# Prompt logits: the low keys of two key chunks in the two partition halves, multiplied by 64 rows each

## The chip, the cores and the metric

The kernel runs on one core of a Trainium2 chip. The metric is the device time of one execution in microseconds; runs of one kernel here lie within 3 us of each other. The engines are named as in the profile: PE (TensorE, matrix products), PEld (its weight loads), DVE (VectorE), ACT (ScalarE), POOL (GpSimd) and SP (SyncE, which here only issues transfers).

## What is computed

One inference step of a decoder layer on a prompt of 2048 tokens and on 8 sample sequences of 4 tokens. The stage that the change touches is stick-breaking attention over the prompt, 8 heads of 64:

```python
def stick_breaking(q, k, v, sb_bias, q_pos, k_pos):
    z = jnp.einsum('bqhd,bkhd->bhqk', q.astype(jnp.float32), k.astype(jnp.float32)) * (HEAD_DIM_SB ** -0.5)
    z = z + sb_bias.astype(jnp.float32)[None, :, None, None]
    mask = k_pos[None, :] < q_pos[:, None]
    log_1mb = jnp.where(mask, jax.nn.log_sigmoid(-z), 0.0)
    suffix = lax.cumsum(log_1mb, axis=3, reverse=True) - log_1mb
    a = jnp.where(mask, jnp.exp(jax.nn.log_sigmoid(z) + suffix), 0.0)
    o = jnp.einsum('bhqk,bkhd->bqhd', a, v.astype(jnp.float32))
    return o.astype(v.dtype)
```

Before it stand the projections to q, k, v and the gated MLP group; after it the output projection, the convolutional feed-forward layer and a per-layer embedding, all in float32.

## The kernel before

Matrix products whose accuracy matters are made of parts: an operand x is split into a high part, x rounded to float32r (a type of 4 bytes that PE multiplies in one pass), and a low part, x minus the high part, also float32r. Elsewhere in the kernel a product is high·high + high·low + low·high (`split_product`, lines 58 to 60).

The kernel is four functions one after the other: `project_mlp`, `project_qk`, `attend` (line 701) and `finish_tokens` (line 1326). `project_qk` writes the transposed queries and keys QT and KT to memory; `attend` writes its result MIXT, which `finish_tokens` loads first.

`attend` runs over 128 steps: 8 heads (`s // NQ`) times 16 query blocks of 128 queries (`s % NQ`, called i). Block i sees 128·(i+1) keys. Keys are taken in granules of up to 1024, which fill one of two PSUM buffers `ps_z` of two banks; blocks 0 to 7 have one granule, blocks 8 to 15 two. Within a granule, chunks of 512 keys (`BANK`) go to one bank each. A chunk narrower than 256 is widened to 256.

How the logits use the 128 rows of PE: a head has only 64 dimensions, so the keys lie twice in the partitions, rows 0 to 63 and again 64 to 127 (`k_hi`, `k_lo`, both 128 x 2048, one slot for each of two heads). `q2` holds the high part of the queries in rows 0 to 63 and the low part in rows 64 to 127. So one product of q2 with k_hi (line 966) gives both high·high and low·high, and one with k_lo (line 967) gives high·low and low·low. Where the chunk holds the diagonal block, a small bf16 product of the identity with a mask (line 970) adds -2^100 to the keys that are not seen. Each matmul has its own load of the 128 query columns as weights.

A step on the engines: PE makes the logits of block t (`logits`), then ACT two sigmoids of each granule (lines 1112 and 1114, into `beta` and `rest`), DVE a running product over the keys (line 1232) and the weights (line 1237); PE transposes the weights of block t-3 (`turn`, line 976), ACT copies them out (`take`, line 1101) and PE multiplies them by V (`weigh`, line 988). Between these, PE does the attention of the sample sequences in units spread over the steps by their estimated cost (`units_of`): transposes of pages of K (line 998), their logits in four column strips of the array (line 1008, `tile_position=(0, 32 * bi)`), and products with pages of V in four column strips (line 1041). POOL loads the pages as PE frees them.

Every engine has its order written out in the program; they meet by semaphores. On PE, `logits` waits for `b_done` (the sigmoids of two granules earlier), and for `half_ready` at blocks 0 (4 in the first head) and 8.

The operands are made for half a head (1024 tokens, number n) at a time. SP loads `k_raw` and `q_raw`, each twice, one copy in each partition half, after `half_ready` reaches n; ACT rounds the keys (`keys_high`); DVE does three parts in three successive steps, beginning with block 10 of the head before (first half) or block 4 of the same head (second half): part 0 rounds the queries (line 1206), part 1 subtracts to make the low rows (line 1209), part 2 makes the low keys (line 1214) and raises `half_ready`. The first 512 tokens of head 0 are made apart (`first_operands`, lines 1222 to 1227).

Of the kernel before, what the change touches and what calls it, by code (L numbers as in the profile page):

```python
# [6 lines left out]
F32R = mybir.dt.float32r  # L7
I32 = mybir.dt.int32
ALU = mybir.AluOpType
# [3 lines left out]
P = 128  # L13
BANK = 512
# [29 lines left out]
def f32(ap):  # L44

    return ap.bitcast(F32)
# [654 lines left out]
def attend(nc, keep, T, D):  # L701
# [10 lines left out]
    HALF, FIRST = 1024, BANK  # L712
# [6 lines left out]
    def keys_of(s):  # L719
        return P * (s % NQ + 1)  # L720
# [4 lines left out]
    def granule(s, g):  # L725
        return sum(granules[:s]) + g
# [56 lines left out]
    for t in range(STEPS + LAG + 1):  # L783
        s = t - LAG
# [6 lines left out]
    with ExitStack() as ctx:  # L791
        m = Alloc(nc, ctx, "at")
        k_raw, q_raw = m.sb("k_raw", [P, HALF]), m.sb("q_raw", [P, HALF])
        k_hi, k_lo, q2 = ([m.sb(f"{n}{s}", [P, 2048], F32R) for s in range(2)] for n in ("k_hi", "k_lo", "q2"))
        v = [m.sb(f"v{s}", [P, NQ, 64]) for s in range(2)]
        beta = [m.sb(f"beta{s}", [P, 2048]) for s in range(3)]
        rest = [m.sb(f"rest{s}", [P, 2048]) for s in range(4)]
# [4 lines left out]
        far_b, ident_b = m.sb("far_b", [P, P], BF16), m.sb("ident_b", [P, P], BF16)  # L802
# [18 lines left out]
        loaded, k_high, q_high, half_ready, z_ready, b_done, product_done, a_done = (  # L821
            m.sem(n) for n in ("loaded", "k_high", "q_high", "half_ready", "z_ready", "b_done", "product_done", "a_done"))
        o_ready, o_out, made, cast, rest_zeroed = (m.sem(n) for n in ("o_ready", "o_out", "made", "cast", "rest_zeroed"))
        first_loaded, first_k_high, first_q_high, first_ready, summed = (
            m.sem(n) for n in ("first_loaded", "first_k_high", "first_q_high", "first_ready", "summed"))
# [41 lines left out]
        with nc.Block() as block:  # L867
# [72 lines left out]
            def _(pe):  # L940
# [7 lines left out]
                def logits(s, g):  # L948
                    i, h = s % NQ, s // NQ
                    n = keys_of(s)  # L950
                    if s == 0:
                        pe.wait_ge(first_ready, 1)
                    if i == (4 if h == 0 else 0) and g == 0:
                        pe.wait_ge(half_ready, 2 * h + 1)
                    if i == 8 and g == 0:
                        pe.wait_ge(half_ready, 2 * h + 2)
                    at = granule(s, g)
                    z = ps_z[at % 2]
                    pe.wait_ge(b_done, at + 1)
                    width = min(n - 1024 * g, 1024)  # L960
                    for c in range(0, width, BANK):
                        w = max(min(BANK, width - c), 2 * P)
                        k0 = 1024 * g + c
                        diagonal = k0 <= n - P < k0 + w
                        q = q2[h % 2][:, i * P:(i + 1) * P]
                        nc.tensor.matmul(z[:, c:c + w], q, k_hi[h % 2][:, k0:k0 + w], start=True, stop=False)
                        last = nc.tensor.matmul(z[:, c:c + w], q, k_lo[h % 2][:, k0:k0 + w], start=False, stop=not diagonal)  # L967
                        if diagonal:
                            d = n - P - 1024 * g
                            last = nc.tensor.matmul(z[:, d:d + P], ident_b[:, :], far_b[:, :], start=False, stop=True)  # L970
                    last.then_inc(z_ready, 1)

                def turn(s, r):
# [103 lines left out]
                for t in range(STEPS + LAG + 1):  # L1077
                    s = t - LAG
                    for g, u in units_of[t]:
                        sample_turns(g, u)  # L1080
                    if has(s):
                        pe.wait_ge(a_done, s + 1)
                        for r in range(first_turns(t)):
                            turn(s, r)
                    if has(t):
                        for g in range(granules[t]):
                            logits(t, g)
                    if has(s):
                        for r in range(first_turns(t), groups[s]):
                            turn(s, r)  # L1090
                    if has(s - 1):
                        weigh(s - 1)
                    for g, u in units_of[t]:
                        sample_products(g, u)
# [104 lines left out]
            def _(dve):  # L1199
                def operands(n, part, first=0):  # L1200
                    slot = n // 2 % 2
                    src = slice(first, HALF)
                    cols = slice(n % 2 * HALF + first, n % 2 * HALF + HALF)
                    if part == 0:
                        dve.wait_ge(loaded, 64 * n + 64)
                        nc.vector.tensor_copy(q2[slot][:, cols], q_raw[:, src]).then_inc(q_high, 1)
                    if part == 1:
                        dve.wait_ge(q_high, n + 1)
                        nc.vector.tensor_tensor(q2[slot][64:P, cols], q_raw[64:P, src], f32(q2[slot][64:P, cols]), ALU.subtract)
                        if n % 2 == 0 and n:  # L1210
                            biases_of(n // 2)
                    if part == 2:
                        dve.wait_ge(k_high, n + 1)
                        nc.vector.tensor_tensor(k_lo[slot][:, cols], k_raw[:, src], f32(k_hi[slot][:, cols]), ALU.subtract).then_inc(half_ready, 1)

                def biases_of(h):
                    nc.vector.tensor_scalar(bias[h % 2][:, :], keep["sb_bias"][:, h:h + 1], 1.0, None, ALU.mult)
                    nc.vector.tensor_scalar(minus_bias[h % 2][:, :], keep["sb_bias"][:, h:h + 1], -1.0, None, ALU.mult)

                def first_operands():  # L1220
                    dve.wait_ge(first_loaded, 64)
                    nc.vector.tensor_copy(q2[0][:, 0:FIRST], q_raw[:, 0:FIRST]).then_inc(first_q_high, 1)
                    biases_of(0)
                    dve.wait_ge(first_q_high, 1)
                    nc.vector.tensor_tensor(q2[0][64:P, 0:FIRST], q_raw[64:P, 0:FIRST], f32(q2[0][64:P, 0:FIRST]), ALU.subtract)
                    dve.wait_ge(first_k_high, 1)
                    nc.vector.tensor_tensor(k_lo[0][:, 0:FIRST], k_raw[:, 0:FIRST], f32(k_hi[0][:, 0:FIRST]), ALU.subtract).then_inc(first_ready, 1)

                def product(s):
                    r = rest[s % 4][:, 0:keys_of(s) - 1][:, ::-1]  # L1230
# [76 lines left out]
                dve.wait_ge(made, 2)  # L1307
                nc.vector.tensor_copy(far_b[:, :], far[:, :]).then_inc(cast, 1)
                first_operands()
                for t in range(STEPS + LAG + 2):  # L1310
                    for g, u in units_of[t]:
                        sample_unit(g, u)
                    if has(t - 1):
                        product(t - 1)
                    if has(t - 2):
                        weights(t - 2)
                    for g, u in units_of[t - 1] if t else ():
                        sample_sums(g, u)
                    if t == 1:
                        for part in range(3):  # L1320
                            operands(0, part, FIRST)
                    for half in range(2):
                        part, h = t % NQ - PART_AT[half], t // NQ + 1 - half
                        if 0 <= part < 3 and h < HEADS:
                            operands(2 * h + half, part)
# [644 lines left out]
def program(nc, T):  # L1970

    D = {n: nc.dram_tensor(n, s, F32, kind="Internal").ap() for n, s in
         (("XT", (1024, 2080)), ("PT", (256, 2080)), ("MIXT", (1024, 2080)), ("QT", (512, 2048)), ("KT", (512, 2048)))}
    with ExitStack() as ctx:
        m = Alloc(nc, ctx, "keep")
        keep = {
            "ident": m.sb("ident", [P, P]), "mean1024": m.sb("mean1024", [P, P]), "mean512": m.sb("mean512", [P, P]),
            "eps": m.sb("eps", [P, 1]), "cols": m.sb("cols", [P, P]), "rs": m.sb("rs", [P, 17]),
            "page_table": m.sb("page_table", [1, P], I32), "sb_bias": m.sb("sb_bias", [P, 8]),
            "qT_s": m.sb("qT_s", [P, 4, 32]), "kT_s": m.sb("kT_s", [P, 4, 32]),  # L1980
        }
        project_mlp(nc, keep, T, D)
        project_qk(nc, keep, T, D)
        attend(nc, keep, T, D)
        finish_tokens(nc, keep, T, D)
# [27 lines left out]
```

## Time and profile before

| | |
|---|---|
| median of 3 runs | 3334.49 us (3333.34 to 3336.3) |
| the profiled execution | 3333.62 us |
| its span in the profile | 3331.6 us |
| mean granted clock of PE in it | 0.982 |
| PE busy | 3181.0 us, 95% |
| DVE busy | 2066.9 us, 62% |
| ACT busy | 1679.9 us, 50% |
| `attend` on PE | 587 to 1330 us of the span |

Times in the profile are microseconds from the start of the span. A row of the view by order of time gives the start, how long the row's instructions take together, engine, line, operation, output and inputs, the shape of the array used (rows*columns), the shape of the streamed operand and the number of instructions run together in the row. PE's matmuls are pipelined: one starts while the one before is still in its tail, so that the distance between starts says what a matmul costs, and the duration says more than that.

### The profile page before, as it was taken

The numbers are of one execution on the slowest core, as the hardware profiler recorded it, in microseconds if no ns is written. First come the engines' busy times: TensorE is split into PE (matmuls) and PEld (weight loads), VectorE is DVE, ScalarE is ACT, GpSimd is POOL, SyncE is SP. The second block draws the span as 40 slices with busy tenths as digits, with TensorE's granted clock in tenths as the row PEclk, the third lists the DMA queues.
The fourth block names the chain that finished last, engine by engine and source line by source line (L and its number), as shares of the span: only waits on it lengthen the run. The fifth ranks groups of instructions, "written<-read, shape, count | busy, mean of one in ns | idle before, by whom it ended". The sixth has DMA issues, their size and how long they took to land.

```text
span 3331.6 us, 52003 instructions
## 1 busy us (share of the span) xinstructions
PE 3181.0 (95%) x18462; PEld 2929.8 (88%) x18462; DVE 2066.9 (62%) x2823; ACT 1679.9 (50%) x2411; POOL 148.3 (4%) x277
## 2 busy tenths in 40 slices
PE   8999899898899889799999999999999999999997
PEld 6888687787678777799999999999999999999997
DVE  4222322777767777577477764777557775678745
ACT  5343211887768767454345443545445543454433
POOL 0000000210311111000000000000000000000000
PEclk9999999999999999899999999999999999999999
DMA  5322333642644333644445334543335433444341
GB/s 170 99 91 74 111 111 101 169 124 74 182 135 122 105 106 97 180 117 118 117 138 149 113 115 116 151 141 113 114 105 178 126 113 116 139 128 119 115 116 59
DMA packets 577751, 405.50 MB, mean 122 GB/s; under 512 B 38025, under 2 KB 539186, under 8 KB 577554
## 3 DMA queue, kind: packets, MB, share of 16 engines
q1 hardware_dynamic: 535172, 298.70, 31.4%
q0 software_dynamic: 20544, 67.19, 7.0%
q10 hardware_dynamic: 21872, 37.39, 3.3%
q8 instruction: 108, 1.77, 0.2%
q14 instruction: 55, 0.45, 0.0%
HBM read 358.34 MB, written 44.87 MB: 121 GB/s over the span
## 4 chain that ended last, share of the span: by engine, by line
PE 57%; ACT 1%; DVE 1%; issue 1%; DMA 0%; ACTq 0%; DVEq 0%
PE pf_acc L60 19%; PE pf_acc L58 19%; PE pf_acc L59 18%; PE pf_ps_sum L1457 0%; DMA pf_mix<-MIXT 0%; ACT pf_c L1635 0%; ACT pf_sq L1582 0%; ACTq L1640 0%; PE pf_ps_t L1494 0%; ACT pf_w_hi L1575 0%; DVE pf_h L1937 0%; DVE pf_u L1744 0%; DVE pf_h L1760 0%; DVE pf_ssum L1754 0%; PE pf_ps_t L1564 0%
## 5 line engine op out<-in xcount | busy, mean ns | idle before, releaser
L60 PE MATMUL pf_acc<-pf_x_hi,pf_w_lo 128*128 128x416 f32 x2080 | 734.2, 353 | 0.0
L1575 ACT ACTIVATE pf_w_hi<-pf_raw 128x1024 fp32r<-128x1024 f32 x440 | 464.6, 1057 | 534.1 <-PE pf_acc L60 528.4
L58 PE MATMUL pf_acc<-pf_x_hi,pf_w_hi 128*128 128x416 f32 x2080 | 732.0, 352 | 1.6 <-issue 0.9
L59 PE MATMUL pf_acc<-pf_x_lo,pf_w_hi 128*128 128x416 f32 x2080 | 725.9, 349 | 0.0
L1738 DVE TENSOR_TENSOR pf_w_lo<-pf_raw,pf_w_hi 128x1024 fp32r<-128x1024 f32 x440 | 536.9, 1221 | 266.6 <-ACT pf_w_hi L1575 266.4
L58 PE MATMUL pf_acc<-pf_f_hi,pf_w_hi 128*128 128x416 f32 x1280 | 454.8, 355 | 8.0 <-DVE pf_w_lo L1738 8.0
L60 PE MATMUL pf_acc<-pf_f_hi,pf_w_lo 128*128 128x416 f32 x1280 | 452.5, 354 | 0.0
L59 PE MATMUL pf_acc<-pf_f_lo,pf_w_hi 128*128 128x416 f32 x1280 | 447.7, 350 | 0.0
L1232 DVE TENSOR_TENSOR_SCAN at_rest<-at_rest 128x127 f32<-128x127 f32 (+15 forms) x128 | 309.8, 2420 | 164.9 <-ACT at_rest L1114 164.7
L59 PEld LDWEIGHTS pf_acc<-pf_x_lo,pf_w_hi 128*128 128x128 f32 x2080 | 390.8, 188 | 8.1 <-issue 1.6
L58 PEld LDWEIGHTS pf_acc<-pf_x_hi,pf_w_hi 128*128 128x128 f32 x2080 | 390.4, 188 | 6.3 <-issue 4.3
L60 PEld LDWEIGHTS pf_acc<-pf_x_hi,pf_w_lo 128*128 128x128 f32 x2080 | 390.0, 188 | 2.2
L988 PE MATMUL at_ps_o<-at_aT,at_v 128*64 128x128 f32 x2176 | 266.8, 277 | 6.0 <-issue 3.5
L988 PEld LDWEIGHTS at_ps_o<-at_aT,at_v 128*64 128x64 f32 x2176 | 236.2, 138 | 21.7 <-issue 11.2
L58 PEld LDWEIGHTS pf_acc<-pf_f_hi,pf_w_hi 128*128 128x128 f32 x1280 | 241.1, 188 | 11.9 <-DVE pf_w_lo L1738 9.2
L59 PEld LDWEIGHTS pf_acc<-pf_f_lo,pf_w_hi 128*128 128x128 f32 x1280 | 241.3, 189 | 5.1 <-issue 1.3
L60 PEld LDWEIGHTS pf_acc<-pf_f_hi,pf_w_lo 128*128 128x128 f32 x1280 | 240.7, 188 | 1.5
L1101 ACT ACTIVATE at_aT<-at_ps_t 128x512 f32<-128x512 f32 (+2 forms) x320 | 160.8, 548 | 58.7 <-PE at_ps_t L976 58.3
L976 PE MATMUL at_ps_t<-keep_ident,at_rest 128*128 128x128 f32 x1088 | 161.3, 284 | 27.5 <-DVE at_rest L1237 24.8
L976 PEld LDWEIGHTS at_ps_t<-keep_ident,at_rest 128*128 128x128 f32 x1088 | 122.9, 145 | 65.0 <-DVE at_rest L1237 38.4
L1112 ACT ACTIVATE at_beta<-at_ps_z,at_bias 128x1024 f32<-128x1024 f32 (+2 forms) x192 | 169.0, 880 | 18.4 <-PE at_ps_z L967 11.9
L58 PE MATMUL pa_ps_acc<-pa_w_hi,pa_x_hi 128*128 128x512 f32 x408 | 165.0, 404 | 6.8 <-DVE pa_w_lo L480 6.8
(226 smaller groups left out, 4404.2 us busy)
## 6 DMA issues: line engine op xcount, KB each, us to landing
pf_raw<-in_w_up_dram SPq DMA_DIRECT2D x220, 512.0 KB, 3.9
pf_raw<-in_w_down_dram SPq DMA_DIRECT2D x80, 512.0 KB, 4.1
at_pages<-in_cache_k_dram POOLq DMA_DIRECT2D x128, 256.0 KB, 3.4
at_pages<-in_cache_v_dram POOLq DMA_DIRECT2D x128, 256.0 KB, 3.3
pf_raw<-in_w_out_dram SPq DMA_DIRECT2D x40, 512.0 KB, 5.5
pf_raw<-in_w_ple_gate_dram SPq DMA_DIRECT2D x40, 512.0 KB, 4.2
pf_raw<-in_w_down_dram SPq DMA_DIRECT2D x40, 384.0 KB, 3.4
pf_mix<-MIXT ACTq DMA_DIRECT2D x5, 1664.0 KB, 8.2
```

Of the source, the lines that this page charges most:

```text
L58: nc.tensor.matmul(out, stat_hi, mov_hi, start=first, stop=False)
L59: nc.tensor.matmul(out, stat_hi, mov_lo, start=False, stop=False)
L60: return nc.tensor.matmul(out, stat_lo, mov_hi, start=False, stop=last)
L976: last = nc.tensor.transpose(bank[:, kt % 4 * P:kt % 4 * P + P], rest[s % 4][:, kt * P:(kt + 1) * P], keep["ident"][:, :])
L988: last = nc.tensor.matmul(ps_o[0:64, i % 4 * P:(i % 4 + 1) * P], v[h % 2][:, kt, :], aT[group(s, r) % SLOTS][:, kt % 4, :], start=kt == 0, ...
L1101: nc.scalar.activation(out, src, ACT.Copy).then_inc(emptied_by(key), 1)
L1112: nc.scalar.activation(beta[t % 3][:, 1024 * g:1024 * g + w], ps_z[at % 2][:, 0:w], ACT.Sigmoid, bias=bias[t // NQ % 2][:, :])
L1232: nc.vector.tensor_tensor_scan(r, r, r, 1.0, ALU.mult, ALU.min).then_inc(product_done, 1)
L1575: nc.scalar.activation(w_hi[k % 4][:, :], raw[k % 4][:, :], ACT.Copy).then_inc(hi_split, 1)
L1738: nc.vector.tensor_tensor(w_lo[k % 4][:, :], raw[k % 4][:, :], f32(w_hi[k % 4][:, :]), ALU.subtract).then_inc(lo_split, 1)
```

## The change

Instead of a second product over all 128 rows for each chunk, the low keys of a granule's two chunks lie in different partition halves: those of keys 0 to 511 of the granule in rows 0 to 63, those of keys 512 to 1023 in rows 64 to 127 (`k_lo` becomes 128 x 2 x 512, indexed by granule). Each is multiplied by the high part of the queries over 64 rows, with `tile_position` (0, 0) and (64, 0). Since rows 64 to 127 of `q2` hold the low part, a rounded copy of the queries is kept in rows 64 to 127 of a new tile, `q_again`. The term low·low is no longer computed. The order within a granule becomes: the high products of both chunks, the low product of the first, that of the second, the diagonal's. Every granule, also one with a single chunk, uses the 64-row form for its low keys. On DVE the low keys are made by two operations of 64 x 512 in place of one of 128 x 1024, and `q_again` by one copy of 64 rows for each half.

```diff
-        k_hi, k_lo, q2 = ([m.sb(f"{n}{s}", [P, 2048], F32R) for s in range(2)] for n in ("k_hi", "k_lo", "q2"))
+        k_hi, q2 = ([m.sb(f"{n}{s}", [P, 2048], F32R) for s in range(2)] for n in ("k_hi", "q2"))
+        k_lo = [m.sb(f"k_lo{s}", [P, 2, BANK], F32R) for s in range(2)]
+        q_again = [m.sb(f"q_again{s}", [P, HALF], F32R) for s in range(2)]
...
-                    for c in range(0, width, BANK):
-                        w = max(min(BANK, width - c), 2 * P)
-                        k0 = 1024 * g + c
-                        diagonal = k0 <= n - P < k0 + w
-                        q = q2[h % 2][:, i * P:(i + 1) * P]
-                        nc.tensor.matmul(z[:, c:c + w], q, k_hi[h % 2][:, k0:k0 + w], start=True, stop=False)
-                        last = nc.tensor.matmul(z[:, c:c + w], q, k_lo[h % 2][:, k0:k0 + w], start=False, stop=not diagonal)
-                        if diagonal:
-                            d = n - P - 1024 * g
-                            last = nc.tensor.matmul(z[:, d:d + P], ident_b[:, :], far_b[:, :], start=False, stop=True)
+                    chunks = [(c, max(min(BANK, width - c), 2 * P)) for c in range(0, width, BANK)]
+                    q, q_high = q2[h % 2][:, i * P:(i + 1) * P], q_again[i // 8][64:P, i % 8 * P:i % 8 * P + P]
+                    d = n - P - 1024 * g
+                    for c, w in chunks:
+                        nc.tensor.matmul(z[:, c:c + w], q, k_hi[h % 2][:, 1024 * g + c:1024 * g + c + w], start=True, stop=False)
+                    for c, w in chunks:
+                        if c == 0:
+                            last = nc.tensor.matmul(z[:, 0:w], q[0:64, :], k_lo[h % 2][0:64, g, 0:w], start=False, stop=not d < w,
+                                                    tile_position=(0, 0))
+                        else:
+                            last = nc.tensor.matmul(z[:, c:c + w], q_high, k_lo[h % 2][64:P, g, 0:w], start=False, stop=not d < c + w,
+                                                    tile_position=(64, 0))
+                    if d < width:
+                        last = nc.tensor.matmul(z[:, d:d + P], ident_b[:, :], far_b[:, :], start=False, stop=True)
                     last.then_inc(z_ready, 1)
...
+                        nc.vector.tensor_copy(q_again[n % 2][64:P, first:], q_raw[64:P, src])
                     if part == 2:
                         dve.wait_ge(k_high, n + 1)
-                        nc.vector.tensor_tensor(k_lo[slot][:, cols], k_raw[:, src], f32(k_hi[slot][:, cols]), ALU.subtract).then_inc(half_ready, 1)
+                        if not first:
+                            low_keys(n, 0)
+                        low_keys(n, 1).then_inc(half_ready, 1)
+
+                def low_keys(n, piece):
+                    slot, rows, at = n // 2 % 2, slice(64 * piece, 64 * piece + 64), BANK * piece
+                    return nc.vector.tensor_tensor(k_lo[slot][rows, n % 2, :], k_raw[rows, at:at + BANK],
+                                                   f32(k_hi[slot][rows, n % 2 * HALF + at:n % 2 * HALF + at + BANK]), ALU.subtract)
...
+                    nc.vector.tensor_copy(q_again[0][64:P, 0:FIRST], q_raw[64:P, 0:FIRST])
                     nc.vector.tensor_tensor(q2[0][64:P, 0:FIRST], q_raw[64:P, 0:FIRST], f32(q2[0][64:P, 0:FIRST]), ALU.subtract)
                     dve.wait_ge(first_k_high, 1)
-                    nc.vector.tensor_tensor(k_lo[0][:, 0:FIRST], k_raw[:, 0:FIRST], f32(k_hi[0][:, 0:FIRST]), ALU.subtract).then_inc(first_ready, 1)
+                    low_keys(0, 0).then_inc(first_ready, 1)
```

## Rows read from the trace of the kernel before

**Rows 1.** The page: the span, and the busy time of each engine.
```profile
span 3331.6 us, 52003 instructions
PE 3181.0 (95%) x18462; PEld 2929.8 (88%) x18462; DVE 2066.9 (62%) x2823; ACT 1679.9 (50%) x2411; POOL 148.3 (4%) x277
```
**Rows 2.** Busy time by stretch: length; PE, PEld, DVE, ACT, POOL; clock; DMA share; GB/s.
```profile
587.00:1309.00 722.00, 664.95 (x5280) 541.39 (x5281) 535.88 (x369) 552.68 (x928) 139.72 (x258) 0.96 0.46 127
...
800.00:850.00 50.00, 41.87 (x294) 33.65 (x294) 47.10 (x35) 37.62 (x58) 7.31 (x14) 0.90 0.32 89
...
1000.00:1050.00 50.00, 49.86 (x429) 42.92 (x427) 38.74 (x21) 42.49 (x73) 7.64 (x15) 1.00 0.39 107
```
**Rows 3.** Waits of PE, 587 to 1309 us: total, times, longest.
```profile
PE at_ps_t L976 <- DVE at_rest L1237: 23.5, 14, 6.9
PE at_ps_t L1041 <- DMA at_pages<-in_cache_v_dram: 22.7, 9, 5.9
PE at_ps_z L966 <- DVE at_k_lo L1227: 12.0, 1, 12.0
```
**Rows 4.** The longest wait of DVE in the same stretch.
```profile
DVE at_rest L1232 <- ACT at_rest L1114: 163.7, 81, 6.8
```
**Rows 5.** The first entry of the chain that ended last: start, length, what.
```profile
1334.51 10.51 DMA pf_mix<-MIXT
```
**Rows 6.** The low-key products by shape: busy and mean ns, idle before.
```profile
L967 PE MATMUL at_ps_z<-at_k_lo,at_q 128*128 128x512 f32 x224 | 90.4, 404 | 0.0
...
L967 PE MATMUL at_ps_z<-at_k_lo,at_q 128*128 128x256 f32 x64 | 18.3, 286 | 0.0
...
L967 PE MATMUL at_ps_z<-at_k_lo,at_q 128*128 128x384 f32 x32 | 11.3, 353 | 0.0
```
**Rows 7.** PE in order of time, one block's logits: start, length, what.
```profile
900.87 0.39 PE L967 MATMUL at_ps_z<-at_k_lo,at_q 128*128 128x512 f32 x1
...
901.57 0.33 PE L966 MATMUL at_ps_z<-at_k_hi,at_q 128*128 128x384 f32 x1
901.74 0.34 PE L967 MATMUL at_ps_z<-at_k_lo,at_q 128*128 128x384 f32 x1
901.92 0.23 PE L970 MATMUL at_ps_z<-at_far_b,at_ident_b 128*128 128x128 bf16 x1
```
**Rows 8.** The same for a block that ends in a 256-column chunk.
```profile
780.44 0.28 PE L966 MATMUL at_ps_z<-at_k_hi,at_q 128*128 128x256 f32 x1
...
780.68 0.23 PE L970 MATMUL at_ps_z<-at_far_b,at_ident_b 128*128 128x128 bf16 x1
```
**Rows 9.** PE and its weight loads where column strips (L1041) follow L988.
```profile
903.22 0.60 PE L988 MATMUL at_ps_o<-at_aT,at_v 128*64 128x128 f32 x4
...
903.55 0.27 PE L988 MATMUL at_ps_o<-at_aT,at_v 128*64 128x128 f32 x1
903.75 1.06 PE L1041 MATMUL at_ps_t<-at_pages,at_rest_s 128*32 128x512 f32 x8
...
903.75 0.16 PEld L1041 LDWEIGHTS at_ps_t<-at_pages,at_rest_s 128*32 128x32 f32 x8 [0.17 <-issue]
```
**Rows 10.** PE around a product of 8 rows (L338) in `project_mlp`.
```profile
27.08 0.27 PE L336 MATMUL pa_ps_o<-keep_ident,pa_ws 128*128 128x128 f32 x1
27.29 0.22 PE L338 MATMUL pa_ps_p<-keep_ident,pa_bs_raw 8*128 8x8 f32 x1
27.44 0.50 PE L58 MATMUL pa_ps_acc<-pa_w_hi,pa_x_hi 128*128 128x512 f32 x1
27.78 0.39 PE L59 MATMUL pa_ps_acc<-pa_w_lo,pa_x_hi 128*128 128x512 f32 x1
```
**Rows 11.** The weight load of the diagonal's product.
```profile
901.91 0.10 PEld L970 LDWEIGHTS at_ps_z<-at_far_b,at_ident_b 128*128 128x128 bf16 x1 [0.15 <-issue]
```
**Rows 12.** DVE's operand lines: ns least, median, most; first and last start; forms.
```profile
L1206 DVE CAST at_q<-at_q_raw x16: 402/686/695, 589.2 to 1250.5; 128x1024 fp32r<-128x1024 f32 x15, 128x512 fp32r<-128x512 f32 x1
...
L1214 DVE TENSOR_TENSOR at_k_lo<-at_k_raw,at_k_hi x16: 691/1217/1221, 590.4 to 1258.4; 128x1024 fp32r<-128x1024 f32 x15, 128x512 fp32r<-128x512 f32 x1
```

## The prediction, made before the changed kernel was run

> **What bounds the kernel now.** I read the page first, then the share of each engine in 50 us stretches, then the instructions of TensorE one by one. The page gives a span of 3331.6 us with PE busy 95% of it [rows 1]. The changed code is the attention stage, `attend`, which runs from 587 us to about 1331 us. Over 587 to 1309 us PE is busy 665 of 722 us, DVE 536 and ACT 553; in a quiet stretch (1000 to 1050) PE is busy 49.9 of 50 us at full clock, and in one with long waits (800 to 850) the granted clock falls to 0.90 [rows 2]. The waits of PE in the stage are few: 23.5 us in 14 waits for the weights from DVE (L1237), 22.7 us in 9 waits for pages of V, 12 us once at the start for the first low keys [rows 3]. DVE meanwhile waits 163.7 us in 81 places for ACT [rows 4], whose sigmoids wait for PE's logits. So PE is the engine whose work sets the length of the stage, and what follows (the projections of `finish_tokens`) starts only when the stage is over: the chain that ended last begins with the load of MIXT at 1334.51 us [rows 5]. A microsecond of PE work in this stage is nearly a microsecond of the kernel.
>
> **What is removed.** A low-key product L967 streams 512, 384 or 256 columns. There are 224, 32 and 64 of these, 320 in all [rows 6], in 192 granules (one in each of the 64 query blocks of number 0 to 7 within a head, two in each of the others). So 128 granules have two chunks. Of the 64 with one chunk, each head has four in its first granule (queries 0 to 3) and four in the second (queries 8 to 11), of widths 256, 256, 384, 512; that is 32, 16 and 16 over 8 heads. The first chunk of a pair is 512 wide. The second chunks are what is left: 224-128-16 = 80 of 512, 16 of 384, 32 of 256. If the two row halves of the array work side by side, a pair costs what its first chunk costs, and the second disappears. Matmuls overlap in their tails, so I take the distance from start to start, not the duration: 0.233 us for 512 columns (900.87 to 901.57 in three steps), 0.175 for 384 (901.57, 901.74, 901.92), 0.12 for 256 (0.24 for the two from 780.44 to 780.68) [rows 7, 8]. Removed: 80 x 0.233 + 16 x 0.175 + 32 x 0.12 = 25.3 us.
>
> Do the halves work side by side? No row here has two row halves. The nearest are the four column strips of L1041: eight matmuls of 512 columns take 1.06 us together [rows 9], where at 0.233 us from start to start eight in a line would take 1.9 us at the least. Strips of the array thus run at the same time. I take the same for row halves.
>
> **What is added on PE: a change of the array's shape, twice a granule.** Each granule now goes from 128-row products to 64-row ones and back. The trace of before has such changes. (a) L338 uses 8 rows: the 128-row matmul ahead of it starts at 27.08, the pitch of 128-column ones of this type is 0.11 (903.22 to 903.55 in three steps [rows 9]), and L338 starts only at 27.29, 0.10 late. Going back, L58 starts with its own weight load at 27.44 instead of having it loaded beforehand, and the next matmul comes after 0.34 instead of 0.23 [rows 10]. (b) From 128x64 to 128x32: 903.55 to 903.75, 0.20 for a pitch of 0.11, 0.09 late; the weight loads behind it show 0.17 us of idle time put down to issue [rows 9]. So a change of shape costs two things, whichever way it goes: 0.09 to 0.10 us in which the array runs empty (I take 0.095, the middle), and the first weight load, which nothing hides: 0.107 us for a 128-column load of these operands (0.34 less 0.233).
>
> The Trainium skill has two rules that pull apart here. TensorEngine Tiling (Array Packing), Key Properties, says that a change of tiling mode drains TensorE while a mere change of tile does not; the two places above agree with it, at 0.09 to 0.10 us each, and by it this change loses. The same page's Overview promises up to 2x for a contraction of 64 rows; by that alone the stage would lose 25.3 us. Its result is rival 1 below.
>
> Per granule: into the 64-row shape, 0.095 + 0.107 = 0.202, 192 times = 38.8 us. Out of it into the diagonal's L970, 128 times: that one's weight load is already not hidden today (0.15 idle before it [rows 11]), so only 0.095, together 12.2 us. Out of it into the next granule's first high product, 64 times (queries 8 to 15 have two granules), 0.202, together 12.9 us. Added: 63.9 us. I count the two weight loads of a pair as parallel, as the strips' are: eight loads of L1041 take 0.16 us [rows 9]. Bounds: if they are serial, 128 x 0.107 = 13.7 us more; if the emptying costs nothing and only the load is exposed, the added sum is 256 x 0.107 = 27.4 us and the change is worth nothing; if both are free for row halves, nothing is added, and less than nothing can't be, since the high products and the diagonal's are all still there.
>
> **What is added on DVE.** `q_again` is a copy of 64 x 1024, like L1206: 0.69 us, 15 times, and 0.40 once [rows 12]. The low keys were one operation of 1024 columns (1.22 us); now they are two of 512 (0.69 each, the short form): 0.16 more, 15 times, and the total is 10.7 + 2.4 = 13 us, or 549 of 722 us. DVE waits 163.7 us for ACT, so most of this is hidden; it counts where PE waits for L1237, 14 times [rows 3, 4]. At the very start nothing hides it: PE waits for the chain of DVE operations that ends in L1227, and the copy of 512 columns stands in it, 0.4 us. I take 1.5 us in all, bounds 0.4 and 13. The copy also holds back the next load by SP (`half_ready` comes 0.85 us later), which is hidden: that load is used four query blocks later at the earliest, blocks of 5.6 us on the mean (722 us for nearly 128). ACT, POOL and SP issue the same work. Moving both high products ahead of both low ones changes nothing that ACT sees, since it waits for the last matmul of the granule.
>
> **What absorbs it.** The net PE cost is 63.9 - 25.3 = 38.6 us in 128 query blocks, 0.3 us each. Where PE waits for something that doesn't depend on how late PE is, a block's share vanishes: 14 + 9 waits of DVE and pages [rows 3], 0.3 us each, at most 7 us. But the longest of them hang on PE themselves (page loads are released by PE's own progress, the long scans by PE's products). I take 5 us. Sum against the profiled execution's 3333.6 us: 3333.6 + 38.6 + 1.5 - 5 = 3368.7. The median shown, 3334.49, is 0.9 us above that execution: 3369.6, so 3370, 1.1% slower.
>
> **Rivals.**
> 1. Row halves need no emptying of the array and their loads are prefetched: only the 25.3 us gain stays. For it: every change of shape in the trace involves columns or 8 rows, none 64 rows at position 64. Against: the 8-row case and the column case show the same price. Time 3334.5 - 25.3 + 1.5 = 3311. Chance 0.10.
> 2. The cost is half (only one of the two parts of each switch is paid, or the emptying overlaps the tail): 63.9 falls to about 25 to 35 us and the gain cancels it. Time 3328 to 3341. Chance 0.08.
> 3. The halves don't overlap (each of the pair streams alone, as when the second must wait for the first): the gain is gone, the switches are all paid: 3334.5 + 63.9 + 1.5 - 7 = 3393. The point from which it decides is the start of the second low product: a few ns after the first, or 0.233 us after it. With only the second load serial it is 13.7 us over my forecast, 3384. Chance of these two together 0.20.
> 4. More of the cost is absorbed: PE has 57 us of idle time in the stage, and if the steps next to each wait give back too, half of the 38.6 us goes: 3334.5 + 19 + 1.5 = 3355. Chance 0.12.
> The forecast as worked out: 0.50.
> The change not doing what it says, that is, both low products landing in the same rows, would be rival 3.
>
> **How the numbers follow.** The likeliest is 3370. Range 3346 to 3394: it takes in rival 4 and all of rival 3, with DVE's bound of 13 us inside it, and leaves out rivals 1 and 2, 18 in 100. 0.2%, about what a measurement of this kernel can tell from no change, is 6.7 us. Faster by more than that 0.11 (rival 1 and the edge of 2), within it 0.07, slower 0.82.
>
> **What the profile after would show.** The two low products of a pair start within 0.01 us of each other and last some 0.4 us. Ahead of the first stands a distance of 0.33 us or so from the last high product instead of 0.23, and the weight-load rows there show idle time put down to issue. L970 starts about 0.33 us after the low products instead of 0.23. The stage ends 34 us later, the busy shares of ACT and DVE in it fall, and the projections after it take as long as before. Wrong would be: a second low product 0.1 or 0.23 us late (rival 3), a first one with no gap (rival 1), a lower granted clock through the quiet stretches (each switch is 0.1 us of emptiness while the trace's drops to 0.90 go with waits of several us, so I expect none), or new waits of PE for L1237 (DVE's 13 us).

## The result, and the profile after

The changed kernel takes 3361.7 us in the median of 5 runs (3356.9 to 3371.2) against 3334.5 us (3331.6 to 3336.3): 1.009 times the time before, 95% interval 1.0073 to 1.0106. It is slower by 27 us. A second measurement, further down, gave 3362.1 against 3334.5, ratio 1.0085 (1.0068 to 1.0102). Executions of one kernel lie further apart here than the 3 us named at the start: 5 us for the kernel before, 14 us for the changed one. The forecast was 3370 with a range of 3346 to 3394.

The page of the changed kernel answers to [rows 1]:

```profile
span 3360.1 us, 52035 instructions
PE 3220.8 (96%) x18462; PEld 2906.9 (87%) x18462; DVE 2080.7 (62%) x2855; ACT 1685.2 (50%) x2411; POOL 149.2 (4%) x277
```

PE is busy for 40 us more with the same 18462 matmuls. Nearly all of the change lies in `attend`: the chain that ended last starts with the load of MIXT 29.0 us later than in [rows 5] (1363.54 to 1334.51), and what comes after it is as long as before.

```profile
1363.54 10.75 DMA pf_mix<-MIXT
```

One query block with two granules, PE in order of time (start, length, what). It answers to [rows 7, 8]:

```profile
902.73 0.71 PE L967 MATMUL at_ps_z<-at_k_hi,at_q 128*128 128x512 f32 x2
903.37 0.50 PE L970 MATMUL at_ps_z<-at_k_lo,at_q 64*128 64x512 f32 x1
903.37 0.49 PE L973 MATMUL at_ps_z<-at_k_lo,at_q_again 64*128 64x512 f32 x1
903.80 0.39 PE L967 MATMUL at_ps_z<-at_k_hi,at_q 128*128 128x256 f32 x1
904.12 0.38 PE L970 MATMUL at_ps_z<-at_k_lo,at_q 64*128 64x256 f32 x1
904.43 0.23 PE L976 MATMUL at_ps_z<-at_far_b,at_ident_b 128*128 128x128 bf16 x1
904.59 1.31 PE L994 MATMUL at_ps_o<-at_aT,at_v 128*64 128x128 f32 x10
```

Three things are to be seen. The two low products of the pair, L970 and L973, start together at 903.37: the row halves do work side by side, and the second product is free. It is so in all 128 pairs of the trace, which start 3 to 4 ns apart. But they start 0.32 us after the second high product, which began at about 903.05 (902.73 + 0.71, less the 0.39 that such a product lasts), where 0.233 was the distance before. And the next high product comes 0.43 us after them: 0.233 of streaming, 0.10 for the weight load that nothing hid, 0.09 to 0.10 in which the array runs empty. The granule of one chunk behind it pays the same on both sides (903.80 to 904.12 and 904.12 to 904.43 where a 256-column product took 0.12) and gains nothing at all.

The weight loads of that block say what ended their idle time:

```profile
903.37 0.18 PEld L970 LDWEIGHTS at_ps_z<-at_k_lo,at_q 64*128 64x128 f32 x1 [0.37 <-issue]
903.37 0.18 PEld L973 LDWEIGHTS at_ps_z<-at_k_lo,at_q_again 64*128 64x128 f32 x1
903.80 0.19 PEld L967 LDWEIGHTS at_ps_z<-at_k_hi,at_q 128*128 128x128 f32 x1 [0.24 <-issue]
```

The two loads of a pair run together as well, and a load of 64 rows of 128 columns takes 0.18 us, nearly as long as one of 128 rows.

Busy time of the stretch from the first logits to the last, which answers to the first of [rows 2], and a quiet stretch, which answers to the last (same columns):

```profile
589.00:1336.00 747.00, 702.46 (x5259) 516.14 (x5260) 547.75 (x399) 555.99 (x925) 140.22 (x257) 0.96 0.45 123
1000.00:1050.00 50.00, 49.69 (x386) 36.49 (x385) 40.07 (x24) 45.68 (x75) 10.00 (x19) 1.00 0.55 144
```

The granted clock is the 0.96 of before, and 1.00 in the quiet stretch. DVE has 12 us more to do in this stretch.

**How the stage is counted from here on.** I took the starts of all matmuls of the stage from the trace, and the distance from each to the next. Where a distance is over 0.25 us longer than is usual for its pair of lines and shapes, the excess is counted as a wait; the rest is work. Work then holds the streams, the weight loads that show, the emptying of the array and the slower clock. Summed over the stage, in us (the median beside it is the kernel's):

| kernel | length | work | waits | median |
|---|---|---|---|---|
| before | 742.8 | 659.2 | 83.6 in 91 places | 3334.5 |
| changed | 770.0 | 698.0 | 71.9 in 86 | 3361.7 |
| e1, 128-row forms | 747.6 | 661.2 | 86.4 in 94 | 3337.7 |
| e2, 64 rows in one half | 785.4 | 720.6 | 64.9 in 81 | 3376.7 |
| e3, one chunk by 128 rows | 756.7 | 678.4 | 78.3 in 87 | 3347.5 |
| e4, a step's high products first | 757.9 | 671.4 | 86.5 in 95 | 3347.2 |
| e5, plain extra work | 768.7 | 699.6 | 69.1 in 76 | 3357.6 |
| e6, wide V, on before | 736.0 | 640.6 | 95.3 in 101 | 3325.8 |
| e7, wide V, on changed | 757.4 | 675.9 | 81.6 in 91 | 3349.9 |
| e8, the best form of the halves | 744.7 | 644.9 | 99.8 in 108 | 3335.4 |
| e9, changed again | 770.8 | 696.5 | 74.3 in 83 | 3362.1 |

The change added 38.8 us of work, where the sum of the forecast had 38.6, and took 11.7 us from the waits: 27.2 us of length. How sharp these figures are can be seen in two ways. Another choice of what is usual (from the lowest tenth of the distances of a pair to their median) moves work and waits of one kernel by 2 to 3 us, and the differences between kernels by up to 1.5. And the two traces of the changed kernel (rows "changed" and "e9") differ by 1.5 us in work and 2.4 in waits. Differences of 1 or 2 us between rows mean nothing.

### The profile page after: what moved, and what is told of

It reads as the page before. It is cut to its first block, busy times and chain, and to the rows that moved or that the text cites. A ratio compares the mean times of both kernels' runs of the same rounds, so it can differ in the third digit from the quotient of the medians.

```text
span 3360.1 us, 52035 instructions
## 1 busy us (share of the span) xinstructions
PE 3220.8 (96%) x18462; PEld 2906.9 (87%) x18462; DVE 2080.7 (62%) x2855; ACT 1685.2 (50%) x2411; POOL 149.2 (4%) x277
## 4 chain that ended last, share of the span: by engine, by line
PE 56%; ACT 1%; DVE 1%; issue 0%; DMA 0%; ACTq 0%; DVEq 0%
PE pf_acc L60 19%; PE pf_acc L58 18%; PE pf_acc L59 18%; PE pf_ps_sum L1472 0%; DMA pf_mix<-MIXT 0%; ACT pf_c L1650 0%; ACT pf_w_hi L1590 0%; ACT pf_sq L1597 0%; PE pf_ps_t L1509 0%; ACTq L1655 0%; DVE pf_h L1775 0%; DVE pf_h L1952 0%; DVE pf_u L1759 0%; DVE pf_ssum L1769 0%; PE pf_ps_sum L1478 0%
## 5 line engine op out<-in xcount | busy, mean ns | idle before, releaser
L982 PEld LDWEIGHTS at_ps_t<-keep_ident,at_rest 128*128 128x128 f32 x1088 | 123.3, 145 | 61.2 <-DVE at_rest L1252 33.3
```

The costliest lines, as they stand in the source:

```text
L982: last = nc.tensor.transpose(bank[:, kt % 4 * P:kt % 4 * P + P], rest[s % 4][:, kt * P:(kt + 1) * P], keep["ident"][:, :])
```

## Experiments

**e1: the same matmuls, all in the 128-row shape.** Does DVE's new work or the new order of the products cost anything by itself? The low keys are left out of the logits here.

```diff
-last = nc.tensor.matmul(z[:, 0:w], q[0:64, :], k_lo[h % 2][0:64, g, 0:w], ..., tile_position=(0, 0))
+last = nc.tensor.matmul(z[:, 0:w], q, k_hi[h % 2][:, 1024 * g:1024 * g + w], ...)
-last = nc.tensor.matmul(z[:, c:c + w], q_high, k_lo[h % 2][64:P, g, 0:w], ..., tile_position=(64, 0))
+last = nc.tensor.matmul(z[:, c:c + w], q, k_hi[h % 2][:, 1024 * g + c:1024 * g + c + w], ...)
```

> The changed kernel with the low products streamed again over all 128 rows (each takes q2 and k_hi as operands, so the low keys are left out of the logits; the number, widths and order of the matmuls are those of the changed kernel). DVE's new copy and the two-piece low keys stay. Theory (the cost is the changes of the array's shape): both the 63.9 us added and the 25.3 us gained go, what is left is DVE's 0.4 to 2 us: 3334.5 + 1.5 = 3336 (3333 to 3340). Rival (DVE's 13 us or the new order of the products, both high ones first, is what cost the time): 3345 to 3362.

Measured: 3337.7 us against 3334.2, ratio 1.001 (1.000 to 1.002). DVE's work and the order together are worth about 3 us (by the interval, 0 to 7). In the table PE's work is 2.0 us longer and its waits 2.8, hardly more than two traces of one kernel differ by. 24 of the 27 us hang on the shape, cost and gain taken together.

**e2: the shape without the halves.** The kernel before, with every low product by 64 rows in rows 0 to 63, behind all high products of the granule.

```diff
-last = nc.tensor.matmul(z[:, c:c + w], q, k_lo[h % 2][:, k0:k0 + w], ...)
+last = nc.tensor.matmul(z[:, c:c + w], q[0:64, :], k_lo[h % 2][0:64, 1024 * g + c:1024 * g + c + w], ...,
...
+                        tile_position=(0, 0))
```

> The kernel before with its low products by 64 rows, all of them in rows 0 to 63, after the high products of the granule: the shapes change as in the changed kernel, but no two products can run side by side, and DVE does what it did before. Theory: 63.9 us added on PE, nothing gained, about 10 absorbed by waits as in the changed kernel: 3388 (3380 to 3396), and in the trace the second low product starts 0.23 us after the first. Rival (the gain of the two halves is not worth its 25 us, or DVE's work is part of the price): about the time of the changed kernel, 3362, or less.

Measured: 3376.7 us against 3334.2, ratio 1.013 (1.0113 to 1.0147): 42 us slower, 15 more than the changed kernel. PE in order of time:

```profile
1003.66 0.71 PE L965 MATMUL at_ps_z<-at_k_hi,at_q 128*128 128x512 f32 x2
1004.31 0.73 PE L967 MATMUL at_ps_z<-at_k_lo,at_q 64*128 64x512 f32 x2
1004.97 0.23 PE L970 MATMUL at_ps_z<-at_far_b,at_ident_b 128*128 128x128 bf16 x1
```

The two low products last 0.73 us together and the second alone 0.39, so that the second starts at 1004.65, 0.34 after the first. That is not the 0.23 that I had written down: the first one's weight load shows (0.10), the second one's is hidden under the first, and between two products of the same 64-row shape the array isn't emptied. From 1004.65 the diagonal's comes after 0.32: 0.233 and the emptying. Work grew by 61.4 us (63.9 in my sum), and waits gave 18.7 back. Against the changed kernel it is 22.6 us of work more: that is what the second stream is worth when it is free, for which the forecast had 25.3. I had expected 3388 and at least 3380; the price of the shapes was right within 3 us, and the share that waits take up was too small (10 us expected).

**e3: granules of one chunk by 128 rows** (but those of head 0's first four blocks).

```diff
+if len(chunks) == 1 and s >= 4:
+    last = nc.tensor.matmul(z[:, 0:w], q, k_lo[h % 2][:, g, 0:w], start=False, stop=not d < w)
-if c == 0:
+elif c == 0:
```

> The changed kernel, but a granule with a single chunk multiplies its low keys over all 128 rows (60 of the 64 such granules; the first four of head 0 stay as they are). Theory: each of the 60 loses 0.202 us on entering and 0.095 on leaving, 17.8 us on PE, some of it absorbed: 3362 - 15 = 3347 (3342 to 3352). Rival (the time went with the pairs, whose order changed): no change, 3358 to 3364.

Measured: 3347.5 us against 3334.2, ratio 1.0047 (1.0030 to 1.0064), 14 us better than the changed kernel. Work went down by 19.6 us (17.8 expected). A little over half of the 27 us came from 60 granules for which the new form could bring nothing.

**e4: half as many changes of shape where a step has two granules.** `logits` is cut in two: with half 0 it makes the high products, with half 1 the low ones and the diagonal's.

```diff
-for g in range(granules[t]):
-    logits(t, g)
+for half in range(2):
+    for g in range(granules[t]):
+        logits(t, g, half)
```

> The changed kernel, but in query blocks of two granules all high products come first and then all low ones, with the first granule's signal at its low products: 64 blocks save one entry and one exit, 0.404 us each, 25.9 us on PE. Theory: 3362 - 22 = 3340 (3335 to 3348). Rival (ACT gets its first granule some 0.9 us later in each such block and hands the delay on): 3350 to 3365.

Measured: 3347.2 us against 3334.2, ratio 1.0042 (1.0026 to 1.0059). Work went down by 26.6 us (25.9 expected), but waits rose by 14.6, so 12 of it arrive in the stage. In the trace, the last low product of a two-granule block's first granule starts 0.99 us after the block's first product instead of 0.65 (medians of 64 blocks): 0.35 us later, not 0.9, while the second granule's comes 0.4 us sooner. The waits of ACT's first sigmoid for the logits grow from 23.7 to 30.7 us in the stage. That is how the rival would show itself; the time lies just inside the range of the theory, and how much of the 14.6 us is this delay no run separates.

**e5: as much plain work, no change of shape.** On the kernel before.

```diff
 nc.tensor.matmul(z[:, c:c + w], q, k_hi[h % 2][:, k0:k0 + w], start=True, stop=False)
+if c == 0:
+    nc.tensor.matmul(z[:, c:c + w], q, k_lo[h % 2][:, k0:k0 + w], start=False, stop=False)
```

> The kernel before with one more product of the first chunk's low keys in each of the 192 granules, in the usual 128-row shape (the low term is added twice, so the logits differ in their last digits): 144 x 0.233 + 16 x 0.175 + 32 x 0.12 = 40.2 us of plain PE work with no change of shape, as much as the changed kernel's logits cost more. Theory (a quarter to three tenths of any PE work added here is taken up by waits that PE has anyway, and that explains the 27 us of the change): 3334 + 29 = 3363 (3358 to 3367). Rival (plain work passes in full, and what fell short in the changed kernel was the price of a change of shape): 3372 to 3376.

Measured: 3357.6 us against 3334.1, ratio 1.0068 (1.0052 to 1.0083). Work rose by 40.4 us, waits fell by 14.5, and the kernel got 23.5 us slower, a little less than the range of the theory had (3358 to 3367). Plain streams are taken up as changes of shape are (14.5 of 40.4 us, against 11.7 of 38.8 and, in e2, 18.7 of 61.4), so the part of the 38.8 us that did not arrive says nothing about the price of a change of shape. In the view of waits, the rows of the weight loads list more of the places than PE's own do (total, times, longest); before, changed, e5:

```profile
PEld at_ps_t L976 <- DVE at_rest L1237: 38.4, 27, 7.2
PEld at_ps_t L1041 <- issue: 30.3, 33, 6.8
```
```profile
PEld at_ps_t L982 <- DVE at_rest L1252: 33.3, 22, 7.4
PEld at_ps_t L1047 <- issue: 25.8, 33, 6.7
```
```profile
PEld at_ps_t L978 <- DVE at_rest L1239: 27.2, 19, 6.9
PEld at_ps_t L1043 <- issue: 26.3, 33, 6.2
```

In both the waits for DVE's weights get fewer, from 27 places to 22 and 19, and smaller in total, from 38.4 us to 33.3 and 27.2. Before the products with V's pages (L1041, L1047, L1043) the places stay 33 and the total falls from 30.3 us to 25.8 and 26.3.

**e6 and e7: take away changes of shape that are there anyway.** If the shape has a price, the kernel before pays it too: its products with V have 64 weight columns and stand between transposes and logits of 128. The weights can be read 128 wide, the neighbour's 64 columns with them, for 64 zero columns more in each of the two buffers; rows 64 to 127 of the result are never read.

```diff
-v = [m.sb(f"v{s}", [P, NQ, 64]) for s in range(2)]
+v = [m.sb(f"v{s}", [P, NQ + 1, 64]) for s in range(2)]
...
-last = nc.tensor.matmul(ps_o[0:64, ...], v[h % 2][:, kt, :], ...)
+last = nc.tensor.matmul(ps_o[:, ...], v[h % 2][:, kt:kt + 2, :].rearrange("p k d -> p (k d)"), ...)
```

> The kernel before with V's weights 128 columns wide (the 64 columns of the key tile and the 64 of the next, a zero pad behind the last; rows 64 to 127 of the result are not read), so that the products with V keep the shape of the transposes and logits around them. Same number of matmuls, same streams. Of the changes of shape in the trace of before 124 entries into 128x64 and 77 exits to 128x128 go (48 exits into column strips stay). Theory (each costs 0.095 empty and 0.05 for the first weight load of these operands): 201 x 0.147 = 29.5 us less on PE, less a quarter: 3334 - 22 = 3312 (3306 to 3320). Rival (the gaps seen there are not the shape's but the sequencer's or a semaphore's): no change, 3330 to 3338.

Measured, on the kernel before: 3325.8 us (10 runs, 3321.9 to 3327.6) against 3334.1 (14 runs), ratio 0.9973 (0.9963 to 0.9982). It is faster than both kernels. The place in the trace, first before, then e6:

```profile
901.92 0.23 PE L970 MATMUL at_ps_z<-at_far_b,at_ident_b 128*128 128x128 bf16 x1
902.08 0.32 PE L988 MATMUL at_ps_o<-at_aT,at_v 128*64 128x128 f32 x1
```
```profile
905.13 0.23 PE L970 MATMUL at_ps_z<-at_far_b,at_ident_b 128*128 128x128 bf16 x1
905.20 2.00 PE L988 MATMUL at_ps_o<-at_aT,at_v 128*128 128x128 f32 x16
```

0.16 us became 0.07: the gap is the shape's, not the sequencer's or a semaphore's. But of the 22 us that I expected only 8 came. Work fell by 18.6 us and not by 29.5; 4.4 of the rest are the products with V themselves, whose starts now lie 0.111 us apart instead of 0.109, 2176 times. Of the other 6, some 3 are a saving that was counted and isn't there: in 58 places the products with V follow the diagonal's product L970, and there the first weight load shows as before (0.160 us from the first to the second before, 0.165 in e6), where the forecast had taken off 0.05 us each. The last 3 us are not placed. And waits rose by 11.7 us, more than half of what was saved. PE's waits for DVE's weights:

```profile
PEld at_ps_t L976 <- DVE at_rest L1237: 43.1, 31, 7.2
```

31 places instead of 27. PE and the chain of ACT and DVE are near a balance in this stage: of work added on PE 64 to 70% arrived in the length of the stage (e5, e2, the changed kernel), of the work removed here 37%. Whether the two directions really differ is not shown: by the medians it is 58% in e5 and 45% here, and with the intervals 43 to 69% and 32 to 66%.

> The changed kernel with the same wide weights of V. Theory (each change of shape has its price by itself, and they add): the same 22 us off 3362: 3340 (3333 to 3347). Rival (a change soon after another is cheaper, as when the array is empty already): less than 12 us off, 3350 and more.

Measured, on the changed kernel: 3349.9 us against 3334.1, ratio 1.0050 (1.0035 to 1.0065), 12 us off the changed kernel's time. Work fell by 22.1 us (20.6 from e9's trace), not less than in e6: the changes of shape have their price each, one soon after another is not cheaper. The time lies between what the two theories gave, again for the waits (9.7 us more of them).

**e8: the row halves at their best.** e4, with blocks 0 to 3 by 128 rows and the wide V.

```diff
+if i < 4 and s >= 4:
+    last = nc.tensor.matmul(z[:, 0:w], q, k_lo[h % 2][:, g, 0:w], start=False, stop=not d < w)
-if c == 0:
+elif c == 0:
```

> The changed kernel with the fewest changes of shape that its layout allows without work of another kind: a step's high products before its low ones, query blocks 0 to 3 (but those of head 0) over all 128 rows, and the wide weights of V. PE work against the kernel before: 63.9 - 25.3 - 25.9 (64 steps x 0.404) - 8.3 (28 x 0.297) = +4.4, and about -25 for the wide weights, so -20 us. Theory (adding or removing work, waits take up a good part, as in the runs with wide weights where 12 of 25 came through): 3334 - 8 = 3326 (3321 to 3334), no better than the kernel before with wide weights alone (3326). Rival (the two-piece use of the array is worth something once the changes of shape are few): 3318 or less.

Measured: 3335.4 us against 3334.5, ratio 1.0004 (0.9994 to 1.0014), not told apart from the kernel before and 10 us behind e6. It is 1 us above the range of the theory, and the rival is out. Work is 14.3 us under that of before (20 expected), but all of it went into waits, 16.2 us more of them, where I had let 8 us come through:

```profile
PEld at_ps_t L995 <- DVE at_rest L1266: 51.9, 37, 7.4
```

**e9: the changed kernel once more.**

> The changed kernel once more, on the chip of the run beside it: 3357 to 3367, with the 64-row pairs starting within 0.01 us of each other as in the first trace.

Measured: 3362.1 us (3360.6 to 3363.9) against 3334.5, inside the range, and all 128 pairs start 3 to 4 ns apart. The first five runs spread over 14 us, these four over 3.

## Why the prediction was right

The direction, the mechanism and the time held: 3370 forecast, 3362 measured, and nearly all of the difference is in one term. The net work, 38.6 us forecast and 38.8 measured, agrees better than its parts do: the price of the shapes came out 2.5 us lower (61.4 for 63.9) and the gain 2.7 us lower (22.6 for 25.3), and e9's trace gives 37.3 for the whole. An agreement to 0.2 us is luck; one to 3 us is not.

**The streams saved, 25.3 us.** The pairs start together, as the column strips of [rows 9] had suggested, and 80 + 16 + 32 products in the second half are there by shape. e2 against the changed kernel gives 22.6 us of work for it (e2 is without DVE's new work and has the new order). Rival 3 (the halves in a line, or their loads) is ruled out by the equal starts, at 903.37 and in the other 127 pairs.

**The changes of shape, 63.9 us.** e2, which has them and no gain, does 61.4 us more work. Each is 0.09 to 0.10 us empty plus 0.10 for the load, as read from two places in the trace of before, one of them a single matmul of 8 rows [rows 10]. Rivals 1 and 2 needed a price near nothing or half of this. (Rival 2's 3328 to 3341 don't follow from its own terms: 25 to 35 us added, less 25.3, plus 1.5 are 3336 to 3346. The measured time is outside both.) One sentence of the forecast had the right sum in the wrong place: I wrote that L970 starts 0.33 us after the low products. The exposed load belongs to the first product of the new shape, so its time shows behind that product: 0.32 in front of the pair (0.233 and the emptying), 0.43 behind it (load, stream, emptying).

**DVE, 13 us more, 1.5 on the path.** The additions are there (`q_again` 11.2 us, low keys 21.9 us instead of 19.7), DVE is at 548 us, and e1 puts the cost together with the new order at 3 us; it doesn't separate the two. New waits of PE for L1237, the sign of DVE's bound of 13 us, did not come: there are fewer of them.

**What absorbs it, 5 us: the term that was mis-sized.** It is 11.7 in the changed kernel (14.5 for e5's plain work, 18.7 in e2). I had capped it at 7 by the 23 waits of PE that [rows 3] lists, one block's 0.3 us for each. Those rows, and the 57 us of idle time that I took from [rows 2], count only the time after the modelled end of a matmul; since a matmul's duration reaches 0.16 us and more past the start of the next (0.39 us for 512 columns, started 0.233 us apart), short waits vanish in it, and longer ones look shorter. Start to start there are 84 us of waits in 91 places. Also, a block's share is not the most that one wait can give. With the waits of two traces set side by side place by place, 22 of them are over 0.3 us shorter in the changed kernel and 22 in e5, and the longest single loss is 1.5 us in e5 (6.5 to 5.0, a product with a page of V) and 3.8 us in the changed kernel (4.4 to 0.6; 1.8 in e9): PE's lateness from several blocks adds up until a long wait takes it. So the sentence that a microsecond of PE's work is nearly one of the kernel was too strong; 0.7 arrived. Rival 4 put the part taken up at half, 19 us; it was three tenths, between the forecast and the rival.

The sum with the measured terms: 38.8 of work less 11.7 is 27.2 us of stage, on 742.8. The first logits come 1.9 us later than before, of which 0.4 is the new copy in DVE's chain; the rest is in `project_qk`, which the change doesn't touch (in e9 the stage starts 0.7 us earlier than in the first trace), and the part after the stage is 0.5 us shorter. Together that is the 28.5 us between the two spans. (The forecast said that the stage would end 34 us later, where its own terms add up to 35; it ended 29.0 us later.)

The granted clock did not move, as forecast.

## What to carry to other kernels

A matmul that uses fewer rows or columns of the array than its neighbours pays for it twice, going in and coming out; before splitting products over parts of the array, count the changes of shape and hold them against the streams saved (here 0.2 us each against 0.233 at best for a pair), and group products of one shape. The reverse is the cheap gain: reading a narrow weight tile as wide as its neighbours cost 2 ns a matmul here and made this kernel 0.27% faster. And measure PE's slack from start to start, for a busy time that includes the tails of matmuls hides the short waits which decide how much of a saving or a cost arrives.

## What the runs showed of the hardware that was not expected

Of 40 us of work put on PE 24 arrived, of 19 us taken off 8, in the medians. A change of the array's shape costs the same 0.09 to 0.10 us for rows (128 to 64: 0.32 us for a pitch of 0.233, 64 to 128: the same in e2, 128 to 8: [rows 10]) and for columns (128 to 64: 0.16 us against 0.07 in e6, 64 to 32: [rows 9]), also where no position in the array is asked for, as in the products with V. Two products of the same 64-row shape in the same half don't pay it, and the second one's weight load is hidden (e2: 0.34 us from the first to the second, of which 0.10 is the first one's load, and 0.32 from the second to the diagonal's).
